# An encoder trunk on one core: norm, h and the opening of a stage by token halves

## The reference

```
def rmsnorm(x, g):
    r = lax.rsqrt(jnp.mean(xf * xf, axis=-1, keepdims=True) + EPS)
    return (xf * r).astype(x.dtype) * g
...
def swiglu(h, w_up, w_down):
    a, b = jnp.split(h @ w_up, 2, axis=-1)
    return (jax.nn.silu(a) * b) @ w_down
...
    mod = (jax.nn.silu(c) @ w_ada + b_ada).reshape(B, N_MOD, 1, D)
    h = rmsnorm(x, norm_g[0]) * (1 + mod[:, 1]) + mod[:, 0]
    x = x + 0.5 * mod[:, 2] * swiglu(h, w_up1, w_down1)
    h = rmsnorm(x, norm_g[1]) * (1 + mod[:, 4]) + mod[:, 3]
...
    x = x + mod[:, 5] * (merged @ w_o)
```

## Time and profile before

| | before |
|---|---|
| time, median of 3 runs | 2609.92 us (2609.33 to 2611.22) |
| profiled execution | 2611.3 us, span 2609.5 us |
| mean granted TensorE clock | 0.979 |
| PE busy | 2468.1 us (95%) |
| DVE busy | 1474.1 us (56%) |
| ACT busy | 745.4 us (29%) |
| POOL busy | 241.8 us (9%) |

### The profile page before, as it was taken

How to read it: one execution, slowest core, us unless ns; L and a number is a source line. 1 busy time by engine, 2 the same in 40 slices (tenths; PEclk the granted TensorE clock), 3 DMA queues, 4 the chain that set the end, 5 groups by cost and what they waited for, 6 DMA issues and landing times.

```text
span 2609.5 us, 42638 instructions
## 1 busy us (share of the span) xinstructions
PE 2468.1 (95%) x19084; PEld 2403.4 (92%) x19084; DVE 1474.1 (56%) x2229; ACT 745.4 (29%) x892; POOL 241.8 (9%) x232
## 2 busy tenths in 40 slices
PE   7899999898899989999989999998889998999997
PEld 3899999888799989999989999998878998999997
DVE  1876777645745587643367777635456556344333
ACT  2312122433322431222241221134233234222222
POOL 1210011101000221000021001011000002000001
PEclk9899999899899999999999999999999999999998
DMA  6654654311123345333236455432112223323321
GB/s 204 185 157 142 175 162 134 93 51 54 55 65 105 94 142 157 111 97 93 67 111 181 144 166 154 122 92 65 56 41 80 82 81 97 82 73 103 92 68 57
DMA packets 401157, 279.91 MB, mean 107 GB/s; under 512 B 10090, under 2 KB 379218, under 8 KB 400846
## 3 DMA queue, kind: packets, MB, share of 16 engines
q1 hardware_dynamic: 379027, 204.73, 27.7%
q0 software_dynamic: 18432, 67.12, 8.4%
q10 hardware_dynamic: 3515, 5.34, 0.6%
HBM read 273.74 MB, written 3.40 MB: 106 GB/s over the span
## 4 chain that ended last, share of the span: by engine, by line
PE 87%; DVE 6%; ACT 4%; issue 1%; DMA 1%; POOL 1%; ACTq 0%; POOLq 0%; DVEq 0%
PE acc L454 76%; PE acc L479 3%; PE ps_mod L509 2%; PE acc L723 2%; ACT w_hi L787 1%; DVE w_lo L1046 1%; PE ps_sum L608 1%; DVE rstd L1121 1%; DMA ada_raw<-in_w_ada 1%; POOL h_lo L383 1%; DVE rstd L1313 1%; ACT h_hi L800 0%; DMA x_in<-in_x_sample 0%; PE ps_sum L542 0%; DVE tmp L1130 0%
## 5 line engine op out<-in xcount | busy, mean ns | idle before, releaser
L454 PE MATMUL acc<-h_hi,w_hi 128*128 128x272 f32 x3648 | 1055.4, 289 | 9.5 <-DVE q L1304 3.6
L454 PE MATMUL acc<-h_lo,w_hi 128*128 128x272 f32 x3648 | 1051.8, 288 | 0.0
L454 PE MATMUL acc<-h_hi,w_lo 128*128 128x272 f32 x3648 | 1051.6, 288 | 0.0
L1046 DVE TENSOR_TENSOR w_lo<-raw,w_hi 128x2048 fp32r<-128x2048 f32 x224 | 512.7, 2289 | 358.5 <-ACT w_hi L787 358.4
L454 PEld LDWEIGHTS acc<-h_hi,w_hi 128*128 128x128 f32 x3648 | 688.5, 189 | 12.8 <-issue 12.0
L454 PEld LDWEIGHTS acc<-h_lo,w_hi 128*128 128x128 f32 x3648 | 688.5, 189 | 0.0
L454 PEld LDWEIGHTS acc<-h_hi,w_lo 128*128 128x128 f32 x3648 | 686.9, 188 | 0.0
L787 ACT ACTIVATE w_hi<-raw 128x2048 fp32r<-128x2048 f32 x224 | 427.7, 1909 | 320.3 <-PE acc L454 210.5
L454 PE MATMUL acc<-u_lo,w_hi 128*128 128x272 f32 x1408 | 404.8, 287 | 0.0
L454 PE MATMUL acc<-u_hi,w_lo 128*128 128x272 f32 x1408 | 404.6, 287 | 0.0
L454 PE MATMUL acc<-u_hi,w_hi 128*128 128x272 f32 x1408 | 403.1, 286 | 0.0
(11 more groups left out here) (171 smaller groups left out, 2505.9 us busy)
## 6 DMA issues: line engine op xcount, KB each, us to landing
raw<-in_w_up SPq DMA_DIRECT2D x176, 512.0 KB, 5.3
ada_raw<-in_w_ada POOLq DMA_DIRECT2D x128, 512.0 KB, 4.2
raw<-in_w_in SPq DMA_DIRECT2D x72, 512.0 KB, 4.6
raw<-in_w_down SPq DMA_DIRECT2D x64, 384.0 KB, 4.2
raw<-in_w_down SPq DMA_DIRECT2D x64, 320.0 KB, 3.4
ada_raw<-in_w_ada SPq DMA_DIRECT2D x16, 512.0 KB, 4.4
raw<-in_w_o SPq DMA_DIRECT2D x32, 256.0 KB, 3.0
raw<-in_w_pool_out SPq DMA_DIRECT2D x16, 256.0 KB, 3.0
```

The source lines that it names most:

```text
L454: last = mm(out, ws(a, kk), xs(b, kk), start=(kk == 0 and n == 0), stop=(kk == nk - 1 and n == 2))
L1046: dve.tensor_tensor(w_lo[p][:, :], raw[p][:, :], f(w_hi[p][:, :]), ALU.subtract).then_inc(w_split, 1)
```

## The change

The last output block of a feed-forward or a middle is finished one token half at a time: PE does half 0's product, then the column sums of blocks 0 to 6 (and block 7's half 0), then half 1's product. DVE adds the block by halves (`half_x`), ACT squares and takes the root by halves, POOL splits the square by halves, DVE inverts by halves. ACT calls Sqrt on one column in advance, so that its table is loaded before. `make_h` runs twice, over 8 half blocks each: half 0 with 272 columns, half 1 with 240 and 32. The four buffers of scaled x are now half blocks in tmp, the squares lie in prod. ACT rounds the second unit's weights between its sixth and seventh half block of h; DVE splits them in two pieces, and takes half 1's reciprocal, between the halves of h. A feed-forward opens with unit 0 on half 0, unit 1 on half 0, unit 0 on half 1, unit 1 on half 1; a middle opens with its first unit on half 0 and then on half 1. The eviction of unit 0's half 0 stands inside the h of half 1. The final norm goes by halves too. The diff, cut:

```diff
+            def turn(first=False, last=False):
+                for n in range(KD if first else KD - 1):
+                    square_part(n)
+                if not first:
+                    square_part(KD - 1, 0, HT)
+                if not last:
+                    odd_h(1)
+                if not first:
+                    square_part(KD - 1, HT, T)
+                if not last:
+                    for q in range(3, 2 * KD, 2):
+                        odd_h(q)
...
+            def unit_half(p, hf, bank, follow=False, second=False):
                 w = w_view(p, "p (b k n) -> p b k n", SLOT, b=2, k=KD)
+                take(bank)
+                if follow:
+                    for kk in range(KD):
+                        hs[kk % 2].step()
+                        pe.wait_ge(h_ready[kk % 2], hs[kk % 2].at())
+                        if kk == 3 and hf == 0 and layers_begun[0]:
+                            column_sum(KD - 1, 1)
                         for b in range(2):
                             for n, (c, d) in enumerate(((0, 0), (0, 1), (1, 0))):
+                                last = mm(acc[:, 2 * bank + b, 0:HT], w[c][:, b, kk, :],
+                                          (h_hi, h_lo)[d][:, kk, cols(hf)],
                                           start=(kk == 0 and n == 0), stop=(kk == KD - 1 and n == 2))
+                else:
+                    for b in range(2):
+                        if second and b:
+                            begin_unit()
+                        last = product(acc[:, 2 * bank + b, 0:HT], lambda a, kk: w[a][:, b, kk, :],
+                                       parts(h_hi, h_lo, hf), KD)
+                done(bank, last)
...
                         if half == 0 and n == 0:
-                            first_unit(0, (todo, place))
-                        else:
+                            begin_unit()
+                            unit_half(0, 0, 0, follow=True)
+                            mods(todo, place)
+                            pe.wait_ge(second_begun, seconds.at(1))
+                            seconds.step()
+                            unit_half(1, 0, 1, second=True)
+                            mods(todo, place + 1)
+                            unit_half(0, 1, 0, follow=True)
+                            mods(todo, place + 2)
+                            unit_half(1, 1, 1)
+                            mods(todo, place + 3)
+                        elif half or n > 1:
...
+                            if half and n == KD - 1 and hf == 0:
+                                done(1, last)
+                                for kk in range(KD - 1):
+                                    column_sum(kk, 0, 1)
+                                column_sum(KD - 1, 0)
...
                     if (kind, n) == MID[0]:
-                        first_unit(slot)
+                        begin_unit()
+                        seconds.step()
+                        unit_half(slot, 0, 0, follow=True)
+                        unit_half(slot, 1, 1, follow=True)
...
+            def last_square(hf):
+                wait_group(1)
+                square(KD - 1, (acc_free[1], pair1.at(1)), hf * HT, (hf + 1) * HT)
+            def turn(s, first=False):
+                if not first:
+                    last_square(0)
+                norm_root(0)
+                if first:
+                    norm_root(1)
+                    copy_rows()
+                for q in (0, 1):
+                    round_h(s, q)
+                if first:
+                    split(0)
+                else:
+                    last_square(1)
+                for q in (2, 3, 4, 5):
+                    round_h(s, q)
+                split(1)
+                for q in (6, 7):
+                    round_h(s, q)
+                if not first:
+                    norm_root(1)
...
+                        if half == 0 and n == 0:
+                            for q in range(KD, 2 * KD):
+                                round_h(s, q)
+                                if q == KD + 2:
+                                    swish(0)
+                            swish(1)
+                            swish(0)
+                            split(0)
+                            swish(1)
+                            continue
...
+            def half_x(hf, s):
+                dve.wait_ge(acc_ready[1], pair1.at(1))
+                pair1.step()
+                for h, a, b, c, g in PARTS:
+                    if h == hf:
+                        last = dve.scalar_tensor_tensor(x[:, KD - 1, c:c + b - a], acc[:, 2 + hf, a:b],
+                                                        coef[:, s, 2, KD - 1, g:g + 1], x[:, KD - 1, c:c + b - a],
+                                                        ALU.mult, ALU.add)
+                last.then_inc(acc_free[1], 1)
+            def split_second():
+                dve.wait_ge(w_rounded, unit.at(1))
+                n = SLOT // 2
+                dve.tensor_tensor(w_lo[1][:, 0:n], raw[1][:, 0:n], f(w_hi[1][:, 0:n]), ALU.subtract)\
+                    .then_inc(second_begun, 1)
+                dve.tensor_tensor(w_lo[1][:, n:SLOT], raw[1][:, n:SLOT], f(w_hi[1][:, n:SLOT]), ALU.subtract)\
+                    .then_inc(w_split, 1)
+                unit.step()
+            def turn(s, before=None):
+                def first_split(q):
+                    if before is None and q == 2:
+                        split(0)
+                if before is not None:
+                    half_x(0, before)
+                reciprocal_root(0)
+                if before is None:
+                    reciprocal_root(1)
+                    dve.wait_ge(rows_turned, 1)
+                    shift_scale(0, 0)
+                else:
+                    half_x(1, before)
+                make_h(s, 0, first_split)
+                split_second()
+                if before is not None:
+                    reciprocal_root(1)
...
+            def ffn(s, todo, last_stage):
+                def evict(n, hf, p):
+                    u_t.step()
+                    dve.wait_ge(acted_ok, u_t.at())
+                    dve.tensor_tensor(prod[:, p, 0, :], acted[:, p, 0, :], acc[:, 2 * p + 1, 0:HT],
+                                      ALU.mult).then_inc(acc_free[p], 1)
+                    pairs[p].step()
+                    freed(p)
+                    two_parts(u_hi[:, n, cols(hf)], u_lo[:, n, cols(hf)], prod[:, p, 0, :], u_ready)
+                def early(q):
+                    if q == KD + 2:
+                        evict(0, 0, 0)
                 for half in range(2):
                     place = half * (2 * HK + KD)
                     for n in range(HK):
+                        if half == 0 and n == 0:
+                            make_h(s, 1, early)
+                            evict(1, 0, 1)
+                            due(todo, place)
+                            due(todo, place + 1)
+                            evict(0, 1, 0)
+                            due(todo, place + 2)
+                            split(0)
+                            evict(1, 1, 1)
+                            due(todo, place + 3)
+                            continue
...
+            half_x(0, 2)
+            reciprocal_root(0)
+            half_x(1, 2)
+            for half in range(2):
+                if half:
+                    reciprocal_root(1)
+                for kk in range(KD):
+                    dve.scalar_tensor_tensor(x[:, kk, cols(half)], x[:, kk, cols(half)], vec_t[:, R_FG + kk:R_FG + kk + 1],
+                                             rstd[:, cols(half)], ALU.mult, ALU.mult).then_inc(h_ready[0], 1)
```

More of the change, by code:

```diff
@@ L369, in _, with odd_h, square_part @@
         def _(pool):
[L370 to L384, removed]
+            rounded, squared = tallies(2)
+            def odd_h(q):
+                kk, half = q % KD, q // KD
+                own = slice(half * HT, (half + 1) * HT)
+                rounded.step(2)
+                pool.wait_ge(h_rounded, rounded.at())
+                pool.tensor_tensor(h_lo[:, kk, own], scaled_x(q), h_hi[:, kk, own].bitcast(F32), ALU.subtract)\
+                    .then_inc(h_ready[1], 1)
+            def square_part(n, a=0, b=T):
+                squared.step()
+                pool.wait_ge(x_squared, squared.at())
+                pool.tensor_tensor(h_lo[:, n, a:b], square_of(n)[:, a:b], h_hi[:, n, a:b].bitcast(F32), ALU.subtract)\
+                    .then_inc(sq_split, 1)
+            def turn(first=False, last=False):
[10 more added lines that the diff above has]
+                        odd_h(q)
             def window_sums(g, layer):
@@ L533, in direct_rows, with column_sum @@
                 ada.step(DIRECT)
[L535 to L544, removed]
+            def column_sum(kk, *hfs):
+                pe.wait_ge(sq_split, squares.at(1))
+                squares.step()
+                for hf in hfs:
+                    for b, part in enumerate((h_hi, h_lo)):
```

(17 more changed lines are left out.)

207 lines of the change are left out of this document (104 added, 103 removed).

## The result

The changed kernel takes 2628.09 us (median of 4 runs, 2626.51 to 2629.32) against 2610.57 for the kernel before: a ratio of 1.0067, 95% interval 1.0052 to 1.0081. It is slower by 17.5 us in the medians and by 15.1 in the two profiled executions (spans 2624.6 and 2609.5). That is inside the range forecast, on the side forecast, and twice the 8.8 of the likeliest case. The kernel before, measured again beside the experiments, took 2611.16 us (1 to 4) and 2611.36 (5 to 7); the changed kernel's 2628.09 is always the figure above. One run of experiment 1 (3020.22 us, its only one with a profile, at a granted clock of 0.757) and one of experiment 3 (6764.44 us) lie far outside the others and stand for nothing here; they move the medians there by less than 0.3 us.

The account below looks back on a forecast made before the run. PE was 95% busy, so only its idle time counted, chiefly 44.0 us waiting for h_lo. Turns +9.4, clock +6.3, end -6.9 made +8.8 on the profiled 2611.3: 2620.1, or 2618.7 as median; range 2603 to 2631.

Parts of the forecast that it names:

- the likeliest case: Whole kernel: slower by 8.8 us on the profiled execution, forecast median 2618.7 us; chance 0.56.
- The moved wait: Feed-forward openings with tiles: tile rows and weight split behind h delay unit 2, 4.3 us later at T3.
- T3: Turn from layer 0 to layer 1, stepped in detail: +4.3 us, plus 2.1 for the clock.
- rival C: Unit 2's weight split doesn't stand in PE's way, no clock lost: -22 us, about 2588; chance 0.15.
- The exclusion between POOL and DVE: Making h: each engine waits out the other's instruction; six turns total +9.4 us with it, -1.8 without.
- POOL's half piece: POOL's split of a half block of h: taken as 0.72 us, between 0.69 and 0.84.
- The clock: Unit 2 after PE's idle stretch runs at lower clock: 2.1 us at each of three turns, +6.3 together.
- the early table load: ScalarE's 1.28 us table load, taken early beside the down units, with no cost counted.
- T0: Turn at the start, opening the first feed-forward: +4.3 us, plus 2.1 for the clock.
- The middles' openings: Turns into the middles: earlier first half but more instructions, so no gain; -0.9 us and +1.8 us.
- T5 and the end: Last turn, without tiles: -3.8 us; final norm and output, transposes starting earlier on half 0: -6.9 us.
- late tiles: adaLN tiles landing a fifth later than 4.1 us after issue: +2.7 us, an upper bound.

Follow-up runs that it names:

- experiment 1: Changed kernel with adaLN tile rows four places later at T3 and the turn out of layer 0's middle: 2607.02 us, ratio to before 0.9982.
- experiment 3: Changed kernel with POOL subtracting only 16 columns of each odd half block of h, the rest not computed: 2611.65 us, ratio to before 1.0002.
- experiment 2: Changed kernel with DVE's weight split for unit 2 put before the adaLN tiles where feed-forwards open, same work: 2597.23 us, ratio to before 0.9953.
- experiment 7: Kernel 6 with DVE splitting the second unit's weights behind both halves of h where a middle opens: 2602.85 us, ratio to before 0.9962.
- kernel 6: Kernel of experiment 2 with the Sqrt table load later and experiment 1's later tiles added: 2595.02 us, ratio to before 0.9940.
- experiment 4: Changed kernel with the last scaling of x in whole blocks after both reciprocals, transposes waiting for all: 2633.17 us, ratio to before 1.0084.

## Why the prediction was right, and where its sizes were off

**The moved wait: right.** Three tiles, an eviction and the split behind h hold unit 2 up: 8.2 us of idle PE at T3 (8.3 forecast). Experiments 1 and 2 take the wait away in two ways, and both gain what the step gives. With the split in front, the kernel does what rival C described: -14 where C gave -22. The pieces found elsewhere in this document would make a little more than these 8 (table load 1.4, the feed-forwards' supply 3.2, the middles' openings 1.4, unit 3 about 3.3). What decides is DVE's order, as C said; as the changed kernel's order stood, unit 2 waited.

**The exclusion between POOL and DVE: right.** The prediction had it at 11.2 us over the six turns (+9.4 with it, -1.8 without). Experiment 3 gained 16.4, which also holds POOL's own shorter time for the odd blocks, 3 by the rival there.

**POOL's half piece: 0.72 was too small.** With DVE idle beside it, it takes 0.76:

```profile
1373.01 0.76 POOL L386 TENSOR_TENSOR h_lo<-tmp,h_hi 128x272 fp32r<-128x272 f32 x1 [1.47 <-ACT tmp L878]
```

By the prediction's own bounds (0.03 us less takes 1.7 off, 0.12 more adds 5) a piece costs some 0.45 us in the six turns for every 0.01 us, so 0.04 makes about 1.8 us. That is an estimate, no run changes this length alone. The six openings together came out some 4.6 later than stepped; what the other 2.8 are isn't separated. At T3 the miss is seen as h's end at 34.9 instead of 34.2 and unit 2 at 50.2 instead of 49.3.

**The clock: right, the size near.** 1.8 + 3.1 + 2.3 = 7.2 against 6.3, with 1.00 in unit 2 at T5 and in experiment 2, where no idle stretch stands in front of it.

**The step that was missing: the early table load.** I had put it at nothing, since it stood "beside the down units". In the other three feed-forwards that holds: the five waits for w_lo are all at the openings and in T0's last down units. In T0's feed-forward tiles are still summed in the last down units, DVE and ScalarE are in a ring of 9.0 us a unit (update, squares, rounding, split, rows) against 8.2 on PE, and 1.28 us more came through as 1.4. The cover that I named was used up there.

**The middles' openings: right in kind, 0.8 and 0.6 low.** The first unit ends 33.9 us after zero at T1, as before, and at 34.2 against 31.9 at T4; the second unit starts at 35.0 against 35.1, and at 35.35 against 33.0. So -0.1 and +2.4 where -0.9 and +1.8 were forecast, and the openings of the middles gain nothing, as I had it. The rest of -2.9 and +5.6 is the clock inside the middles (last section): -2.8 and +3.2. Nothing of the edit stands there, and that the two nearly cancel is luck.

**T5 and the end: right** to 0.9 and 0.3.

**The range.** It was widened upwards for POOL's half (+5), the clock (+3) and late tiles. The first two made about 2.7, and the tiles landed 4.2 us after they were asked for, as forecast; the table load, the middles and the rest of the supply were not in it, and the time lies 3 us under its upper end. That it held is in part luck.

The profiled executions account for 15.1. The other 2.4 of the medians' 17.5 lie between runs of the same kernel (spans of 2624.6, 2624.8, 2627.5 and 2627.5); which stage they come from isn't known, as the runs without a profile don't tell.

## What to carry to other kernels

When a start is made earlier by splitting work into halves, follow the queue of each engine to the next unit and ask what stands in front of what that unit needs; work that used to hide under a unit (here the tiles' rows) must be moved behind the next weights. Where two engines hold each other up, as DVE and POOL do here (0.50 us alone, 1.00 beside POOL), small pieces cost more than their instruction count: count each by its time beside the other engine. A short piece of work put behind a long one in a queue can hold up an engine that needs only the short one (experiment 7). A piece of work called free has to be checked in each stage for itself, since cover that is there in three stages was gone in the fourth.

## What was not expected of the hardware

The same stretch of the same code has two durations, by the granted clock. The middle from just behind its second unit on, with the same work, in windows of the kernel before (layer 0, layer 1) and of the changed one (layer 0, layer 1), with a second stretch, later in the middle, below each:

```profile
543.60:597.70 54.10, 48.69 (x353) 44.19 (x352) 22.57 (x47) 14.53 (x27) 3.60 (x4) 0.97 0.21 62
1807.60:1860.10 52.50, 47.09 (x352) 43.39 (x352) 22.56 (x47) 14.54 (x26) 3.55 (x4) 1.00 0.22 64
703.40:729.70 26.30, 23.76 (x162) 23.18 (x161) 19.65 (x22) 11.24 (x12) 0.00 (x0) 0.81 0.22 62
1965.80:1990.80 25.00, 21.77 (x161) 21.39 (x160) 19.62 (x22) 11.23 (x11) 0.00 (x0) 0.93 0.23 65
```

```profile
551.20:603.70 52.50, 47.08 (x352) 43.36 (x351) 22.58 (x47) 14.51 (x26) 3.54 (x4) 1.00 0.22 64
1829.60:1883.80 54.20, 48.78 (x352) 44.15 (x352) 22.58 (x47) 14.53 (x26) 3.54 (x4) 0.97 0.21 62
709.40:734.40 25.00, 21.74 (x161) 21.37 (x160) 19.62 (x22) 11.28 (x11) 0.00 (x0) 0.93 0.23 65
1989.50:2016.00 26.50, 23.25 (x161) 22.88 (x160) 19.63 (x22) 11.28 (x11) 0.00 (x0) 0.87 0.22 61
```

At 1.00 the first stretch takes 52.5 us, at 0.97 54.1 to 54.2, and the layers change places between the kernels. In kernel 2 both layers have the slower one (54.1 and 54.3), in kernel 7 both the faster (52.6, against 54.3 and 54.2 in kernel 6). The second stretch does the same: 25.0 us at 0.93 here, 26.0 to 26.5 at 0.80 to 0.87. That this needs no cause in the program is seen in experiment 4, whose program is the changed kernel's up to the end. The second stretch of its layer 0 is not:

```profile
709.00:735.40 26.40, 23.17 (x162) 22.79 (x160) 19.64 (x22) 11.24 (x12) 0.00 (x0) 0.87 0.22 62
```

From the same start to the end of the middle, all kept traces but experiment 1's take 353.9 to 358.5 us. So a single profile of this kernel may differ from another by several us in each middle without a cause in the change, and kernels within a few us of each other can't be told apart by one trace. What decides which duration comes is open.
